# Gate products among the chunk matrices, the router stage by halves, and the last expert outside the loops of a hybrid RWKV-7 / GLA / mixture-of-experts block

## The reference

```python
u = rmsnorm(h, norm_mix[i])
proj = u @ w_in[i]
y_rw = rwkv7_mix(token_shift(proj[..., :RW_COLS], shift_mu[i]), ...)
y_gla = gla_mix(proj[..., RW_COLS:], ...)       # o = norm(o) * norm_g * silu(g)
h = h + concatenate([y_rw, y_gla], axis=-1) @ w_out[i]
u = rmsnorm(h, norm_ffn[i])
logits = u @ w_router + b_router                # (256, 32)
top_v, top_i = top_k(logits, 4); gates = softmax(top_v)
# each expert e, for its tokens:
hgl = xb @ w1[e] + b1[e]                        # w1[e]: 1024 x 2048
act = (clip(hgl[:, D_FF:], -7, 7) + 1) * (x_glu * sigmoid(1.702 * x_glu))
out[tokens] += (act @ w2[e] + b2[e]) * gate     # w2[e]: 1024 x 1024
h = h + sigmoid(rmsnorm(h, norm_ple[i]) @ w_ple_gate[i]) * (p[i] @ w_ple[i])
return rmsnorm(h, norm_final)
```

## Time and profile before

| | |
|---|---|
| median of 3 runs | 1248.39 us (1244.37 to 1248.87) |
| profiled execution | 1249.29 us, span 1247.6 us |
| mean granted clock | 0.979 of full speed |
| TensorE busy | 1162.5 us (93%) |
| VectorE busy | 345.3 us (28%) |
| ScalarE busy | 225.7 us (18%) |
| GpSimd busy | 56.9 us (5%) |
| moved by DMA | 431.99 MB, mean 346 GB/s over the span |
| expert chunks | 2048 KB each, six per expert |
| chain that ended last | TensorE 56%, DMA 37%, VectorE 4% |

### The profile page before, as it was taken

The page is one execution under the profiler, slowest core; times in us unless marked ns, Lnnn a source line. Parts: engine busy times, 40 slices in busy tenths (PEclk is TensorE's granted clock), DMA queues, the critical chain, the costliest instruction groups (busy, mean ns, idle before and its releaser), DMA issues.

```text
span 1247.6 us, 14604 instructions
## 1 busy us (share of the span) xinstructions
PE 1162.5 (93%) x5623; PEld 550.3 (44%) x5623; DVE 345.3 (28%) x756; ACT 225.7 (18%) x402; POOL 56.9 (5%) x102
## 2 busy tenths in 40 slices
PE   6999799997999999899999999999999999999996
PEld 5877698652333333333333333333333333333342
DVE  1361864631222223222222222222322222222232
ACT  3233121111121111111111111111111121111123
POOL 7003700000000000000000000000000000000000
PEclk9999899988999999999999999999999999999999
DMA  9400103885999999999999999999999999999950
GB/s 325 171 1 20 41 2 150 335 319 226 423 429 429 429 428 428 429 429 429 428 428 429 429 429 429 429 429 429 429 429 429 428 427 429 428 429 429 429 234 34
DMA packets 41811, 431.99 MB, mean 346 GB/s; under 512 B 5268, under 2 KB 8664, under 8 KB 16664
## 3 DMA queue, kind: packets, MB, share of 16 engines
q1 hardware_dynamic: 41784, 431.63, 82.6%
HBM read 430.57 MB, written 1.05 MB: 346 GB/s over the span
## 4 chain that ended last, share of the span: by engine, by line
PE 56%; DMA 37%; DVE 4%; issue 1%; ACT 1%; SPq 0%; POOL 0%; DVEq 0%; ACTq 0%
PE ps L1143 52%; DMA ring<-in_w_dram 37%; DVE t L1084 1%; PE ps L1157 1%; PE ps L1558 1%; DVE ring L866 1%; PE ps L1510 1%; PE ps L1358 1%; DVE ay L1097 0%; DVE ay L1093 0%; PE ps L1568 0%; DVE ring L871 0%; DMA xb<-in_x_dram 0%; DVE ay L1089 0%; PE ps L1244 0%
## 5 line engine op out<-in xcount | busy, mean ns | idle before, releaser
L1143 PE MATMUL ps<-ring,ay 128*64 128x512 f32 x1024 | 242.3, 616 | 37.4 <-DMA ring<-in_w_dram 35.0
L1143 PE MATMUL ps<-ring,gqk 128*64 128x512 f32 x1024 | 224.6, 596 | 9.1 <-issue 5.8
L1079 DVE COPY t<-ps 128x512 f32<-128x512 f32 x32 | 22.1, 692 | 524.2 <-PE ps L1143 524.2
L1143 PEld LDWEIGHTS ps<-ring,ay 128*64 128x64 f32 x1024 | 72.6, 140 | 181.9 <-issue 136.4
L1143 PEld LDWEIGHTS ps<-ring,gqk 128*64 128x64 f32 x1024 | 78.9, 138 | 151.7 <-issue 146.1
L702 ACT ACTIVATE t<-ps 128x512 f32<-128x512 f32 x32 | 19.1, 597 | 367.0 <-PE ps L1143 367.0
L1143 PE MATMUL ps<-ring,bu 128*128 128x512 f32 (+1 forms) x224 | 83.8, 533 | 1.1 <-DVE bu L759 1.0
L1143 PE MATMUL ps<-bu,ring 128*128 128x256 f32 (+2 forms) x328 | 69.5, 374 | 1.0 <-DVE bu L757 1.0
L1143 PE MATMUL ps<-lg,gqk 128*64 128x512 f32 x256 | 61.4, 622 | 5.8 <-issue 5.8
L1143 PE MATMUL ps<-yb,ohgt 64*128 64x512 f32 x264 | 65.6, 615 | 0.1
L1143 PEld LDWEIGHTS ps<-bu,ring 128*128 128x128 f32 (+1 forms) x328 | 60.2, 191 | 11.0 <-DVE bu L757 1.4
(11 more groups left out here) (295 smaller groups left out, 921.3 us busy)
## 6 DMA issues: line engine op xcount, KB each, us to landing
ring<-in_w_dram SPq DMA_DIRECT2D x128, 2048.0 KB, 24.3
lg<-in_w_dram SPq DMA_DIRECT2D x16, 2048.0 KB, 25.9
ka<-in_w_dram SPq DMA_DIRECT2D x16, 2048.0 KB, 28.3
bu<-in_w_dram SPq DMA_DIRECT2D x16, 2048.0 KB, 29.2
bkv<-in_w_dram SPq DMA_DIRECT2D x16, 2048.0 KB, 31.2
ring<-in_w_in_dram SPq DMA_DIRECT2D x5, 2048.0 KB, 17.5
ring<-in_w_out_dram SPq DMA_DIRECT2D x1, 4096.0 KB, 12.8
ring<-in_w_ple_gate_dram SPq DMA_DIRECT2D x1, 4096.0 KB, 33.8
```

The lines of the kernel that those rows point to most:

```text
L1079: dve.tensor_copy(HS[:, 512:1024].rearrange("p (j q) -> p j q", j=4), bank(5).rearrange("p (q j) -> p j q", j=4)).then_inc(hs1, 1)
L1143: return pe.matmul(out_, lhs, rhs, start=start, stop=stop, skip_group_check=shared)
```

## The change

- The gate products are cut into eight parts (`gg_part`), one behind each unit of chunk matrices, which come in another order (`MAT_ORDER`). `TAB` is gone: VectorE makes `X_` for a unit in one operation from banks 6 and 7, which every unit uses (`tab_ok`), and GpSimd has two operations per unit instead of three.
- The router's weights are scaled by the norm's gain once, on VectorE, and the turned sum is copied without scaling.
- The first bias is loaded on a semaphore of its own and transposed behind the output projection's `k` = 4 to 7. SyncE issues two `w1` chunks right after it.
- The last products of the output projection are cut in four parts, and the transposes of the first tokens and of half of the second ones stand between them. The logits are made transposed, four products side by side in 32 columns each (`logit_parts`), and a product with `ID4` adds the four parts up. The top four are picked for each half of the tokens by itself (`select`), and `open_sums` stands where selections and positions are waited for. The first gather matrix is made before the gates.
- `item` of TensorE is cut into `w1_stage` and `w2_stage`. The first expert's `w1_stage` stands before the count is read and the loop entered; the loop runs `w2_stage` of one expert and `w1_stage` of the next.
- The last pair of experts (on VectorE and ScalarE the last expert) stands outside the loops. Its last `w2_stage` has no gather and no turn, and transposes its scatter matrix ahead of the down-projection instead of in its middle.

The diff, cut to its core:

```diff
+MAT_ORDER = (2, 3, 4, 5, 6, 7, 0, 1)
+MAT_BANKS = ((4, 5), (2, 3))
+GG_ORDER = ((0, 1), (1, 1), (0, 0), (1, 0))
...
+            load_cols(6, 0, 1, RWC + 2 * GQ + GV_W + 256, 256)
+            sp.wait_ge(gg_ps, 3)
...
+            sp.wait_ge(b1_ps, 1)
+            load_w1(1, 1, 3)
+            load_w1(0, 0, 3)
...
-            for c in range(2, W1C):
-                load_w1(0, 0, c)
-            sp.wait_ge(lg_ps, 1)
+            load_w1(0, 0, 2)
+            sp.wait_ge(lg_ps, 3)
             load_w1(1, 1, 2)
-            sp.wait_ge(b1_ps, 1)
-            load_w1(1, 1, 3)
...
+            for n, u in enumerate(MAT_ORDER):
                 m2 = slice(2 * u, 2 * u + 2)
-                pool.wait_ge(mat_ok, u + 1)
-                link(pool.tensor_tensor(X_[:, m2, :], TAB[:, m2, :], D1L[:, :].unsqueeze(1).broadcast_to([P, 2, P]), ALU.mult))
+                pool.wait_ge(mat_ok, n + 1)
...
+                with act.Fori(0, NE - 1) as e:
                     for b in range(nb):
                         item(e * nb + b)
+                for b in range(nb):
+                    item((NE - 1) * nb + b, b == nb - 1)
...
+            dve.wait_ge(small_in, 16 * 7)
+            link(dve.tensor_tensor(WR3, WR3, col("norm_ffn", 0, KC).unsqueeze(2).broadcast_to([P, KC, NE]), ALU.mult), tok_v)
...
+                signal(dve.tensor_tensor(X_[:, m2, :], bank(6, 2).rearrange("p (j w) -> p j w", j=2)[:, :, 0:P],
+                                         D1L[:, :].unsqueeze(1).broadcast_to([P, 2, P]), ALU.mult), tab_ok)
                 for j in range(2):
-                    m = 8 * t + 2 * h + j
-                    signal(dve.tensor_tensor(MT[:, m, :], bank(b0 + j), mk1, ALU.mult))
-                    signal(dve.tensor_tensor(TAB[:, m, :], bank(b0 + 2 + j)[:, 0:P], SL[:, :], ALU.mult))
+                    signal(dve.tensor_tensor(MT[:, 2 * u + j, :], bank(b[j]), mk1, ALU.mult))
...
+            dve.wait_ge(wout_ps, 1)
+            signal(dve.tensor_tensor(XB3[:, 0, :], bank(4, 2), XB3[:, 0, :], ALU.add), scaled)
+            dve.wait_ge(wout_ps, 2)
+            signal(dve.tensor_tensor(XB3[:, 1, 0:512], bank(6), XB3[:, 1, 0:512], ALU.add), scaled)
+            dve.wait_ge(xt_ps, 2 * KC + 2)
+            dve.tensor_copy(UT3[:, 4:8, 0:P], bank(1).rearrange("p (k w) -> p k w", k=4)).then_inc(ut_v, 1)
+            dve.wait_ge(xt_ps, 2 * KC + 3)
+            dve.tensor_copy(UH, bank(2).rearrange("p (k w) -> p k w", k=4)).then_inc(ut_v, 1)
...
+            def select(t):
+                dve.wait_ge(lg_ps, 2 * t + 2)
+                link(dve.scalar_tensor_tensor(out=lg[:, t, 0:NE], in0=bank(6 + t)[:, 0:NE], scalar=SM[:, 24 + t:25 + t],
+                                              in1=BR[:, :], op0=ALU.mult, op1=ALU.add))
+                link(dve.max(top[:, t, 0:8], lg[:, t, 0:NE + 4]))
+                signal(dve.tensor_scalar(SM[:, 100 + t:101 + t], top[:, t, 0:1], -1.0, None, ALU.mult), lg_max)
+                link(dve.memset(top[:, t, 4:8], NEG))
+                link(dve.match_replace(mr[:, t, 0:NE + 4], top[:, t, 0:8], lg[:, t, 0:NE + 4], 2 * NEG))
+                signal(dve.tensor_tensor(ms[:, t, 0:NE], mr[:, t, 0:NE], lg[:, t, 0:NE], ALU.not_equal), sel_ok)
...
-            pe.wait_ge(win[6], 16)
-            pe.wait_ge(win[7], 16)
-            for t in range(TT):
-                pe.wait_ge(tok_a, t + 1)
-                for half, s in ((0, 11), (1, 0)):
-                    for k in range(KC):
-                        ins = mm(bank(t)[:, 256 * half:256 * (half + 1)], UT3[:, k, P * t:P * (t + 1)], cols(s, 256)[:, k, :],
-                                 k == 0, k == KC - 1)
-                ins.then_inc(gg_ps, 1)
...
+                if n:
+                    pe.wait_ge(tab_ok, n)
...
+            def gg_part(n):
+                t, half = GG_ORDER[n // 2]
+                w = cols(0 if half else 11, 256)
+                for k in range(4 * (n % 2), 4 * (n % 2) + 4):
+                    ins = mm(bank(t)[:, 256 * half:256 * (half + 1)], UT3[:, k, P * t:P * (t + 1)], w[:, k, :], k == 0, k == KC - 1)
+                if n in (3, 5, 7):
+                    ins.then_inc(gg_ps, 1)
+            for n, u in enumerate(MAT_ORDER):
+                mats(n, u)
+                gg_part(n)
...
+            pe.wait_ge(b1_in, 16)
+            for i in range(16):
+                c0 = 512 * (i // 4) + i % 4
+                ins = pe.transpose(bank(2)[:, NE * i:NE * (i + 1)], B1R[0:NE, c0:c0 + 512 - i % 4:4], ID[0:NE, 0:NE])
+            ins.then_inc(b1_ps, 1)
...
+            def w_out_rest(t, half, ks):
+                for k in ks:
+                    ins = w_out_product(k, t, half)
+                return ins
+            def turned(t, ks, b):
+                for n, k in enumerate(ks):
+                    ins = pe.transpose(bank(b)[:, P * n:P * (n + 1)], paired(XB3[:, t, :], k), ID[:, :])
+                ins.then_inc(xt_ps, 1)
+            def logit_parts(t, first):
+                for g in range(4):
+                    u = UH[:, g, :] if t and not first else UT3[:, first + g, P * t:P * (t + 1)]
+                    ins = mm(bank(4 + t)[32 * g:32 * g + 32, 0:P], WR3[:, first + g, :], u,
+                             first == 0, first == 4, True)
+                return ins
+            def open_sums(t):
                 for half in range(2):
-                    for k in range(4):
-                        ins = w_out_product(k, t, half)
-                ins.then_inc(wout_used if t else wout_ps, 1)
+                    mm(bank(2 * t + half), OHGT[:, 0:P], XB3[:, t, 512 * half:512 * (half + 1)], True, False, True)
+            ms = RT8[3]
+            w_out_rest(0, 0, range(4))
+            w_out_rest(0, 1, range(4)).then_inc(wout_ps, 1)
+            w_out_rest(1, 0, range(4)).then_inc(wout_ps, 1)
+            pe.wait_ge(scaled, 1)
+            turned(0, range(4), 0)
+            turned(0, range(4, 8), 1)
+            w_out_rest(1, 1, range(2))
             pe.wait_ge(scaled, 2)
-            transposes(XB3, pairs=True)
-            pe.wait_ge(ut_a, 14)
-            pe.wait_ge(ut_v, 10)
-            for t in range(TT):
-                o = bank(6)[:, NE * t:NE * (t + 1)]
-                for k in range(KC):
-                    ins = mm(o, UT3[:, k, P * t:P * (t + 1)], WR3[:, k, :], k == 0, k == KC - 1)
-            ins.then_inc(lg_ps, 1)
-            def open_sums(t):
-                for half in range(2):
-                    ins = mm(bank(2 * t + half), OHGT[:, 0:P], XB3[:, t, 512 * half:512 * (half + 1)], True, False, True)
-                ins.then_inc(zero_ps, 1)
+            pe.wait_ge(b1_ok, 1)
+            turned(1, range(4), 2)
+            w_out_rest(1, 1, range(2, 4)).then_inc(wout_used, 1)
+            pe.wait_ge(tok_v, 5)
+            pe.wait_ge(ut_a, 11)
+            pe.wait_ge(ut_v, 7)
+            logit_parts(0, 0)
+            logit_parts(0, 4).then_inc(lg_ps, 1)
+            pe.wait_ge(ut_v, 8)
+            logit_parts(1, 0)
+            pe.wait_ge(lp_ok, 1)
+            mm(bank(6)[:, 0:NE], LP[:, 0], ID4).then_inc(lg_ps, 1)
+            pe.wait_ge(scaled, 3)
+            turned(1, range(4, 6), 3)
+            turned(1, range(6, 8), 0)
+            pe.wait_ge(ut_a, 12)
+            pe.wait_ge(ut_v, 9)
+            logit_parts(1, 4).then_inc(lg_ps, 1)
+            pe.wait_ge(lp_ok, 2)
+            mm(bank(7)[:, 0:NE], LP[:, 1], ID4).then_inc(lg_ps, 1)
             open_sums(0)
-            pe.wait_ge(brow_in, 48)
-            for i in range(16):
-                c0 = 512 * (i // 4) + i % 4
-                ins = pe.transpose(bank(5)[:, NE * i:NE * (i + 1)], B1R[0:NE, c0:c0 + 512 - i % 4:4], ID[0:NE, 0:NE])
-            ins.then_inc(b1_ps, 1)
             pe.wait_ge(sel_ok, 1)
-            ms = RT8[3]
-            mm(bank(7)[:, 0:NE], SU[:, :], ms[:, 0, 0:NE])
-            mm(bank(7)[:, NE:2 * NE], ONES[:, :], ms[:, 0, 0:NE], True, False)
-            mm(bank(7)[:, NE:2 * NE], SU[:, :], ms[:, 1, 0:NE], False, True)
-            mm(bank(7)[:, 2 * NE:3 * NE], ONES[:, :], ms[:, 0, 0:NE], True, False)
-            mm(bank(7)[:, 2 * NE:3 * NE], ONES[:, :], ms[:, 1, 0:NE], False, True).then_inc(pos_ps, 1)
+            mm(bank(4)[:, 0:NE], SU[:, :], ms[:, 0, 0:NE])
+            mm(bank(4)[:, NE:2 * NE], ONES[:, :], ms[:, 0, 0:NE], True, False)
+            pe.wait_ge(sel_ok, 2)
+            mm(bank(4)[:, NE:2 * NE], SU[:, :], ms[:, 1, 0:NE], False, True).then_inc(pos_ps, 1)
+            mm(bank(5)[:, 0:NE], ONES[:, :], ms[:, 0, 0:NE], True, False)
+            mm(bank(5)[:, 0:NE], ONES[:, :], ms[:, 1, 0:NE], False, True).then_inc(pos_ps, 1)
             open_sums(1)
...
+            gather_turn(0)
...
-            gather_turn(0)
-            pe.wait_ge(gt_ok, 1)
-            pe.wait_ge(cnt_ok, 1)
-            pe.wait_ge(b1_ok, 1)
-            def item(i, h, odd):
+            def w1_stage(i, h, odd):
...
+            def w2_stage(i, h, odd, last=False):
+                if not last:
+                    pe.wait_ge(oh_ok, i + 2)
```

(27 more changed lines are left out.)

231 lines of the change are left out of this document (123 added, 108 removed).

## The result

The kernel after takes 1227.47 us (median of 4 runs, 1225.47 to 1230.69) against 1247.52 us (median of 4 of the kernel before, 1244.37 to 1248.87). The ratio is 0.9843, with a 95% interval from 0.9827 to 0.986. That is 20 us faster, where the forecast sum was 13.5. The profiled execution of after took 1230.69 us, the slowest of its four, with a span of 1229.0 us, 18.6 less than before.

The account below looks back on a forecast made before the run. The prediction took the expert weights' uninterrupted stream as the bound, its end set by the first release. 16.9 us earlier release - 5.2 hole + 1.8 tail = 13.5 us, so 1235.5 us, range 1227 to 1245.

Parts of the forecast that it names:

- Part 1: Gate products mixed among the chunk matrices, TensorE the bound: first level near 140.5 us, 6.7 us earlier (bounds 4 and 8).
- Part 2: First bias's transposes moved ahead of the output projection's last product: cost 2.1 us there, gain 2.1 later, nothing in sum.
- Part 3: Router by halves, from last projection products to first expert product: 42.9 us falls to 31.5, gain 9.3 (6.3 to 11.3).
- my allowance for the clock: In the router stage, 2 us added to 29.5 us at full clock, giving 31.5.
- The release delay: From first expert product to first release of weight room: 4.8 us, a gain of 0.9 (0 to 2.2).
- Part 4: Jump between the first expert's two projections: next release 24.8 us behind, stream stands still 5.2 us (nothing to 9).
- Part 5: Last expert outside the loops, without gather and turn, its down-projection running through: 1.8 us off the tail.
- idle time of TensorE at the last pair: Sign named in advance: the prediction is wrong if TensorE idles at the last pair of experts; no size given.
- Hidden jump: Rival: TensorE's sequencer reaches the branch while products are queued, so the stream doesn't stand still; 1230 us, chance 0.12.
- The small front: Rival about the gain ahead of the stream, its description left out of the text given; chance 0.18.
- The stream doesn't take the gain: Rival: the DMA queue's own sequencer isn't through its branch by 278 us; chance 0.12.
- Fetches behind weights: Rival: instruction fetches wait behind queued weight transfers, jump +11 us, last pair's code +12; 1258 us, chance 0.06.

Follow-up runs that it names:

- e1: Kernel after with the gate products as one block ahead of the chunk matrices again; 7.6 us above the kernel after.
- e5: Kernel after with the two weight chunks that wait for the bias loaded last, in their old places; median 1.3 us above the kernel after, in another set.
- c1: The kernel after run once more, unchanged, in the second set; median 1229.94 us.
- e2: Kernel after with the first expert's up-projection behind the count's read and the jump again, on TensorE alone; 5.4 us above the kernel after.
- e6: Kernel after with both openings of the accumulators moved behind the first gather; median 1231.79 us.
- e9: Kernel after with logits made as before, 32 columns a product and tokens as stationary side, in the new places; median 1233.23 us.
- e4: Kernel after with the last products of the output projection in one block and twelve transposes behind them; 0.6 us below c1.
- e2b: The same kernel as e2, run again beside c1; 3.1 us above c1.
- e7: Kernel after with TensorE's two loop copies swapped, the used one directly behind the test, and the last stage in both; ratio 0.9803 to the kernel before.
- e3: Kernel after with the last expert's unused gather and turn made again, still outside the loops; 1227.56 us against 1227.47.
- e10: e7 with the first expert's up-projection behind the jump again; median 3.5 us above e7, which ran in another set.

## Why the prediction was right, and where it was off

The forecast of the end was 1235.5 us, 1227 to 1245; measured 1227.47, at the lower edge of the range. The case that came is the forecast one: a release that is earlier, a hole behind it, a full stream, a shorter tail. Against the profiled execution's 18.6 us the sum of 13.5 was 5.1 short, nearly all of it ahead of the first release (22.0 where 16.9 were forecast).

- **Part 1, chunk matrices: right.** Forecast 6.7 us, first level at 140.5; measured 7.7 and 139.51. A mixed unit took 3.21 us where 3.27 were reckoned, bound by TensorE as forecast, which makes 0.6 of the 1.0 us. Another 0.5 is at the end of the stage: the 4.05 us for the key transposes and what follows them were read in a stretch of before in which its clock was low (0.89 granted from 142.25 to 146.3 us), and they took 3.52. The prediction didn't divide the gain; e1 does, into 4.7 us of mixing and 3.2 of lighter work, and my expectation for e1 was wrong, since it took the old pace of 2.4 us for the lighter units. The 16 changes between 64-row and 128-row products cost nothing that shows: eight units took the sum of their rows (0.97 + 0.31 + 1.93 us between starts), with no idle time at a change.
- **Part 2, the bias transposes:** 2.10 us ahead of the zero point (2.1 forecast), and the chunks that load earlier are worth nothing, by e5.
- **Part 3, the router by halves: the mechanism was right, and this term was mis-sized.** "The gain is 42.9 - 31.5 - 2.1 = 9.3 us" measured 42.9 - 28.2 - 2.1 = 12.6. Of the 3.3 us, 2.0 are my allowance for the clock. It was my estimate, and no run shows a term of 2 us: in after TensorE stayed at full clock to the end of the stage and lost nothing. That is in part luck, since in c1, the same kernel, the clock fell there and 1.7 us were lost. The other 1.3 or 1.4 us are in the terms up to the second summing product: 20.35 forecast, 260.14 - 241.16 = 18.98 measured. The first logits start 15.32 us behind zero (15.65 forecast); the twelve products side by side took 0.081 and 0.10 us each instead of 0.14 and are over by 16.2 (17.3 forecast); copies and sums took 2.8 instead of 3.05. From the openings to the first expert product it was 9.2 us, as reckoned (29.5 - 20.35 = 9.15). What makes up the 12.6 us: 5.6 are the jump, moved behind the up-projection (e2), 1.7 the openings in the waits (e6, its idle time alone), 1.0 the narrow logits (e9) and 0.5 the split of the projection (e4). The rest wasn't taken apart.
- **The release delay,** from the first expert product to the first release: forecast 4.8 us, a gain of 0.9; measured 3.89, a gain of 1.8. The 4.8 was my estimate, and no run shows it: it is 3.88 or 3.89 us in the eleven executions in which the clock held under the first products, 6.27 and 6.33 with the idle time back ahead of them (e2, e2b), 5.72 before. Release 273.26 instead of 278.4: 7.7 + 12.6 + 1.8 = 22.1 us against 16.9.
- **Part 4, the jump: the hole came, and its size is in part luck.** Forecast next release 24.8 us behind, hole 5.2; measured 23.69 and 4.6. I had put the whole 5.80 us at the jump and named "5 to 6 us" of idle time as a sign; it is 3.09 us of idle time. The near agreement comes from a term that I didn't have, a gather and transposes at the lower clock behind it (3.37 + 1.30 us instead of 1.92 + 1.09, 1.7 in all); together 4.75. (The 6.1 us in the sum stand without a working.) The sum gave the jump the same price in its new place, and that isn't so: by the columns it costs 8.0 us ahead of the first product and 4.7 behind it. And I had counted the read of the count into the price: e7 shows that under products it costs nothing and the fetch of the far target is the whole, to be had by swapping the copies.
- **Part 5, the last expert:** forecast 1.8 us, measured 1.9 from the last up-projection to the end (77.2 to 75.3), and 1.5 by e3. The down-projection starts 0.87 us earlier behind the last up-projection's start (0.85 forecast) and runs through in 7.09 us. I had named idle time of TensorE at the last pair as a sign of being wrong; it is there, 2.79 us ahead of the last up-projection, but it was there before too (2.57), so the sign was badly chosen.
- **The sum:** 22.0 - 4.6 + 1.9 = 19.3, where the span fell by 18.6. The last up-projection starts 16.7 us earlier and the stream ends 17.4 earlier; the 0.7 between them is of the size of the stretches by which I read the stream's end, and I didn't follow it up.
- **The range:** the bounds of the parts as they stand give 1225 at the lower end (8 + 11.3 + 2.2 + 1.8 us, no hole), not 1227. Measured was 1227.47, and 1229.94 in c1, inside either way.

**The rivals.** Hidden jump: dead, as the stream stands still in after, and the instruction packet moves only when the products ahead of the jump are through. The small front (0.18 among the chances): dead, as parts 1 and 3 gave 20.3 us where 16.0 were forecast; the granted clock does fall to 0.5 in the router stage in c1, e1, e2, e2b, e6 and e10. The stream doesn't take the gain: SyncE issued at 273.26, 3.89 us behind the first product, so it was through its branch; dead. Fetches behind weights: with four transfers queued the far jump took 3.09 us of idle time, where this rival needed some 17, and less than the 4.8 us that the distance costs in the empty stretch of e2; at the last pair there is no gap but the wait for the weights; dead.

**What stays open.** Why the clock falls in some executions of the same kernel and not in others; the records give when it falls, not why there. Whether the openings in the waits keep it up. Why the far target costs 4.8 us ahead of the up-projection and 3.1 behind it. And where the clock fell in the longest executions of e9.

## What to carry to other kernels

Find what the release of the first room waits for, and move work from ahead of it to behind it: where the stream runs full once it runs (428 GB/s here) and what the room doesn't hold is still to be moved, that moment and any hole behind it set the end (907.2 to 907.9 us after it without a hole), and the order of the loads ahead of it changed nothing (e5). Where a kernel has two copies of a loop, put the one that runs directly behind the test; that brought 3.5 to 3.7 us here, on top of about 3 for moving the jump behind other work. And give TensorE work that is needed anyway in the waits for small selections, which was worth the 1.7 us of the pause; a fall of the clock behind a pause cost 1.7 us here too, but doesn't come each time (behind 7 of 11 pauses of 2.8 to 2.9 us at the last up-projection).
